# A transformer-like layer with gathered experts: the slots at which TensorE's pieces, the copies of its results and the choices are issued

## What is computed

```python
proj = rmsnorm(x, g_mix) @ w_in            # q | k | v | g (retention) | B | C | h (convolution)
o, ret_new = retention(ret_state, q, k, v) # chunked, with decay
c = gb * short_conv(gc * hc)
x = x + concat([rms_scale(o) * silu(g), c]) @ w_out
# peer: 8 heads; per token and head, 16 of 16,384 experts
q = rmsnorm(x, g_ffn) @ wq
s1, s2 = q[first half] @ keys1.T, q[second half] @ keys2.T
v1, i1 = top_k(s1, 16); v2, i2 = top_k(s2, 16)
top_s, sel = top_k(v1[:, None] + v2[None, :], 16); gate = softmax(top_s)
y = x + sum(gate * gelu(x . u[eidx]) * v[eidx])
y = rmsnorm(y, g_fin)
```

## Time and profile before

| what | value |
|---|---|
| median of 3 runs | 3299.9 us (3294.3 to 3301.84) |
| the profiled execution's own time | 3302.18 us, of which span 3300.4 us |
| first dot product, last dot product | 208.5 us, 3283.1 us |
| PE, DVE, ACT, POOL busy | 73%, 65%, 49%, 36% of the span |
| mean granted TensorE clock | 0.813 |
| moved by DMA | 1223.47 MB, mean 371 GB/s |

### The profile page before, as it was taken

One profiled execution on the slowest core, in us unless ns is written; L12 is line 12 of the kernel. 1 busy time (PEld: TensorE's weight loads), 2 busy tenths in 40 slices (PEclk: granted clock), 3 DMA queues, 4 the chain that ended last, 5 costly groups with the idle time before them and its releaser, 6 DMA issues.

```text
span 3300.4 us, 36101 instructions
## 1 busy us (share of the span) xinstructions
PE 2423.8 (73%) x12644; PEld 1993.6 (60%) x12644; DVE 2141.7 (65%) x6141; ACT 1607.1 (49%) x2626; POOL 1176.6 (36%) x1060
## 2 busy tenths in 40 slices
PE   8867787787776777787776887777766766667766
PEld 7656666656665666666665666655555655555555
DVE  1368875557888644556888744555788888555554
ACT  1135544455455544455455544456455455564455
POOL 0022333344443443334444333234443443444332
PEclk9978888797878888787878999888877777666666
DMA  6269998899999999899999999899999999999997
GB/s 238 79 255 358 375 374 328 310 403 402 415 387 416 383 420 394 317 388 401 418 395 414 369 421 408 320 340 373 419 403 374 366 384 367 412 417 421 421 421 320
DMA packets 183318, 1223.47 MB, mean 371 GB/s; under 512 B 21088, under 2 KB 26400, under 8 KB 43616
## 3 DMA queue, kind: packets, MB, share of 16 engines
q0 software_dynamic: 152064, 1107.36, 83.4%
q1 hardware_dynamic: 31072, 113.80, 9.1%
HBM read 1216.23 MB, written 4.86 MB: 370 GB/s over the span
## 4 chain that ended last, share of the span: by engine, by line
PE 39%; DVE 24%; DMA 18%; ACT 15%; issue 4%; POOL 0%; SPq 0%; DVEq 0%; ACTq 0%; POOLq 0%
DMA ring<-in_uv,idx 17%; PE expert_sum L813 14%; DVE ring L1094 10%; ACT ring L610 8%; PE mm L760 7%; PE mm L669 5%; PE mm L675 5%; PE x_ps L729 3%; DVE pairs_left L977 1%; ACT L621 1%; ACT dots L621 1%; DVE top_i L986 1%; DVE top_i L976 1%; PE tp L770 1%; DVE top_v L984 1%
## 5 line engine op out<-in xcount | busy, mean ns | idle before, releaser
L813 PE MATMUL expert_sum<-ident_sb,ring 128*128 128x128 f32 x8448 | 1486.3, 337 | 827.4 <-ACT ring L610 814.7
L474 POOL DMA_INDIRECT ring<-in_uv,idx x1056 | 1176.4, 1114 | 2094.6 <-PE expert_sum L813 1831.5
L813 PEld LDWEIGHTS expert_sum<-ident_sb,ring 128*128 128x128 f32 x8448 | 1235.1, 175 | 1086.2 <-ACT ring L610 1033.9
L1094 DVE CUSTOM_DVE_ANT_0 ring<-ring,xn 128x1024 f32<-128x1024 f32 x1056 | 1288.4, 1220 | 462.9 <-DMA ring<-in_uv,idx 454.5
L610 ACT ACTIVATE ring<-ring,weights 128x1024 f32<-128x1024 f32 x1056 | 1197.5, 1135 | 0.0
L621 ACT ACTIVATE dots<-dots 128x1 f32<-128x1 f32 x1056 | 211.5, 200 | 1065.2 <-DVE dots L1094 1061.9
L1076 DVE TENSOR_TENSOR weights<-dots,gate 128x1 f32<-128x1 f32 x1056 | 166.0, 157 | 166.5 <-ACT dots L621 166.2
L669 PE MATMUL mm<-stream,xn_in 128*128 128x256 f32 (+1 forms) x1024 | 255.6, 407 | 6.2 <-DVE xn_in L848 6.2
L760 PE MATMUL mm<-turn,stream 128*128 128x256 f32 (+1 forms) x1024 | 256.7, 407 | 0.7 <-ACT turn L554 0.7
L669 PEld LDWEIGHTS mm<-stream,xn_in 128*128 128x128 f32 (+1 forms) x1024 | 198.0, 199 | 47.8 <-DVE xn_in L848 6.6
L760 PEld LDWEIGHTS mm<-turn,stream 128*128 128x128 f32 x1024 | 204.8, 205 | 36.4 <-ACT turn L554 1.1
(11 more groups left out here) (158 smaller groups left out, 1541.7 us busy)
## 6 DMA issues: line engine op xcount, KB each, us to landing
stream<-in_w_ret SPq DMA_DIRECT2D x32, 1024.0 KB
stream<-in_wq SPq DMA_DIRECT2D x32, 1024.0 KB
stream<-in_w_conv SPq DMA_DIRECT2D x24, 1024.0 KB
ring<-in_uv,idx POOLq DMA_INDIRECT x1056
w_out_sb<-in_w_out SPq DMA_DIRECT2D x1, 4096.0 KB, 16.1
x<-in_x SPq DMA_DIRECT2D x8, 512.0 KB
out_y<-xn SPq DMA_DIRECT2D x8, 512.0 KB
xn_in<-in_xT SPq DMA_DIRECT2D x24, 128.0 KB
```

The costliest lines, as they stand in the source:

```text
L474: pool.indirect_dma_start(ring[:, g % RING, :], None, uv, bass.IndirectOffsetOnAxis(ap=rows, axis=0)).then_inc(landed[g % RING], 16)
L813: ins = pe.matmul(expert_sum[:, c * P:(c + 1) * P], ring[:, g % RING, D + c * P:D + (c + 1) * P], ident_sb[:, :], is_transpose=True, start ...
L1094: dve.tensor_tensor_reduce(u, u, xn[:, t % 3, :], 1.0, 0.0, ALU.mult, ALU.add, dots[:, g % RING:g % RING + 1]).then_inc(dotted, 1)
```

## The change

Only slot numbers change, with the order in which choices are made. The sums, sizes and buffers stay, except that the scores of SAMPLE get a place of their own in `qkvg`.

- A projection piece is issued over three slots (matmuls 0 to 2, 3 to 5, 6 and 7), every 4 slots; a query piece two matmuls a slot, its second half 4 slots behind the first. The four parts of retention's last products go to four slots.
- ScalarE and VectorE take a result two slots behind the end of its piece (before: one slot behind its only slot).
- Mixing has 22 slots for a tile (before 18) and begins 24 slots behind the first convolution piece in groups 1 and 2, 4 in groups 0 and 3.
- Heads of group 3 come every 15 slots (before 21), and SAMPLE's choices all behind those of tiles 6 and 7.

```diff
-RET_AT, RET_EVERY = 20, 9
-CONV_AT, CONV_EVERY = 92, 3.5
-MIX_AT, MIX_EVERY = 94, 18
-OUT_AT, OUT_EVERY = 138, 12
+USE_AT, USE_EVERY = 24, 4
+MIX_EVERY = 22
+def conv_at(j):
+    return base_of(j) + USE_AT + USE_EVERY * RET_UNITS * len(GROUPS[j])
+def mix_at(t):
+    j = group_of(t)
+    return conv_at(j) + (24 if j in (1, 2) else 4) + MIX_EVERY * place(t)
+def out_at(t):
+    j = group_of(t)
+    return max(mix_at(t) + 22, conv_at(j) + USE_EVERY * CONV_UNITS + 2 + 10 * place(t))
+def turn_at(t):
+    j = group_of(t)
+    return out_at(ORDERS[j][-1]) + 12 + 3 * place(t)
 def head_at(j, h):
     if j == 0:
-        return 13 * h - 18
-    return turn_at(j, len(GROUPS[j])) + 2 + (15 if len(GROUPS[j]) == 2 else 21) * h
+        return 13 * h - 26
+    return turn_at(ORDERS[j][-1]) + 5 + 15 * h
 def choose_at(j, h, i):
-    return head_at(j, h) + 5 + 7 * i
+    if GROUPS[j][i] == SAMPLE:
+        return choose_at(j, PH - 1, i - 1) + 7 * (h + 1)
+    return head_at(j, h) + 13 + 7 * i
...
         # TensorE, projection(j)
         for k in range(KC):
+            yield slot + k // 3
             ins = pe.matmul(bank[:, 0:w], item[:, unit % 2, k, :], xnj[:, k, :],
...
         # TensorE, queries(j)
-                yield head_at(j, h) + s
+                yield head_at(j, h) + 4 * s
         for k in range(KC):
+            yield head_at(j, h) + 4 * s + k // 2
             ins = pe.matmul(query_bank(j, s), weight[:, s, k, :], xnT_of_group(j)[:, k, :],
...
-                yield choose_at(j, h, i) - 2
+                yield head_at(j, h) + 10 + 7 * i if t < SAMPLE else head_at(j, h) + 13
...
         # ScalarE, projection(j); VectorE, conv(j) likewise
-                    yield slot + 1
+                    yield slot + 4
...
         # ScalarE, queries(j)
-                    yield head_at(j, h) + 2
+                    yield head_at(j, h) + 9
...
         # VectorE, choices(j)
-                for h in range(PH):
-                    for i, t in enumerate(GROUPS[j]):
+                pairs_of_tiles = [(h, i) for h in range(PH) for i in range(2)]
+                if SAMPLE in GROUPS[j]:
+                    pairs_of_tiles += [(h, 2) for h in range(PH)]
+                for h, i in pairs_of_tiles:
```

More of the change, by code:

```diff
@@ L100, in uses_of @@
         for i, t in enumerate(GROUPS[j]):
-            out.append(("ret", u, t, base_of(j) + RET_AT + RET_EVERY * u + RET_EVERY * i // len(GROUPS[j])))
+            out.append(("ret", u, t, base_of(j) + USE_AT + USE_EVERY * (u * len(GROUPS[j]) + i)))
     for v in range(CONV_UNITS):
-        out.append(("ChB"[v % 3], v, None, base_of(j) + CONV_AT + int(CONV_EVERY * v)))
+        out.append(("ChB"[v % 3], v, None, conv_at(j) + USE_EVERY * v))
     return out
@@ L152, in batches_of @@
         return [(0, 1), (2, 3), (4, 5), (6, 7)]
+    if t == SAMPLE:
+        return [(0, 7)]
     return [(0, 3), (4, 7)]
-GATES = sorted((j, last, i, first) for j in range(4) for i, t in enumerate(GROUPS[j]) for first, last in batches_of(t))
+GATES = sorted(((j, last, i, first) for j in range(4) for i, t in enumerate(GROUPS[j]) for first, last in batches_of(t)),
+               key=lambda b: pick(*b[:3]))
 def gates_ready(t, h):
@@ L261, in xn_of, with scores_of @@
             return xn[:, t % 3, :] if t < SAMPLE else xn_in[:, D:2 * D]
+        def scores_of(t, h):
+            if t < SAMPLE:
+                return scores[:, :, :]
+            return qkvg[:, 0, h * 2 * NK:(h + 1) * 2 * NK].rearrange("p (s k) -> p s k", s=2)
         def state_of(t):
@@ L440, in store_states @@
                 j = len(GROUPS) - 1
-                yield base_of(j) + OUT_AT
+                yield out_at(SAMPLE)
                 sp.wait_ge(tails_ready, 2 * CH)
@@ L518, in retention @@
                 n, r, j = rows_of(t), RANK[t], group_of(t)
-                at = base_of(j) + MIX_AT + MIX_EVERY * place(t)
+                at = mix_at(t)
                 yield at
@@ L540, in out @@
                 n, r, j = rows_of(t), RANK[t], group_of(t)
-                at = base_of(j) + OUT_AT + OUT_EVERY * place(t)
-                yield at + 9
+                at = out_at(t)
+                yield at + 10
                 act.wait_ge(x1_ready, r + 1)
@@ L731, in out @@
                 ins.then_inc(wout_done, 1)
-                yield turn_at(j, place(t))
+                yield turn_at(t)
                 pe.wait_ge(xn_ready, r + 1)
@@ L996, in choices @@
                                 dve.wait_ge(keyed_copied, c + 1)
-                            best16(tv[:, s, :], ti[:, s, :], scores[0:n, s, :], left[0:n, s * NK:(s + 1) * NK],
-                                   c + 1 if s else None)
+                            best16(tv[:, s, :], ti[:, s, :], scores_of(t, h)[0:n, s, :], left[0:n, s * NK:(s + 1) * NK],
+                                   pick(j, h, i) + 1 if s and t < SAMPLE else None)
                         yield at + 2
```

102 lines of the change are left out of this document (53 added, 49 removed).

## The result

The changed kernel takes 3121.45 us (median of four runs, 3118.02 to 3123.0) against 3300.87 us: ratio 0.9458, interval 0.9442 to 0.9474. The profiled execution has a span of 3121.2 us and a granted clock of 0.839 (before 0.813).

What follows compares the result with a forecast made beforehand. The prediction took gathers and weight loads (DMA) as the bound, with engine waits for pieces as excess. Gains 73 + 21 - 5 + 31 + 3 = 123 us from 3302 gave 3179, stated as 3178; range 3130 to 3265.

Steps and rivals of the forecast that it cites:

- The bound, and the rule to read a stage by: All slot stages: gathers at 2.52 us a slot plus 2.5 us per 1 MB of weights; time above is excess.
- Term 1: Mixing stages: waits for pieces mostly go, 3.0 us a slot; 73 us gained after 3 us back in each group.
- term 4: Choices: late query copies give 16 us in groups 1 and 2, group 3 gains 18, SAMPLE costs 3; together 31.
- the time ahead of slot 0: Before the first slot, more piece work ahead of TensorE's wait for `gated`: gain 3 us, bounds 0 and 6.
- Terms 2 and 3: First stage gains 21 us from spaced, spread pieces; weights loaded late, mostly in group 1, cost 5 us over all groups.
- the landing: Late weights: a load lands in 8 us against two slots, about 6 us, so each TensorE wait is 2 us.
- Ring buffers cover half: Late weights: ring buffers hide half of TensorE's waits for loads, leaving a cost of 5 us.
- the stage from 1857.6 us: Prepared stage to 2036.9 us, 64 slots and about 7 items: 179 us by the sum, took 179.3.
- The bank whose slack is gone: Rival: pieces behind slot 0 wait for the previous piece's copy, making the kernel slower, for example 3333 us; chance 0.06.
- The clock: Rival: thin parts lower TensorE's clock, making the kernel slower; at 0.55 it takes 3485 us; chance 0.04.
- Gain mostly spent again: Rival: late loads cost 84 us, or choices and mixing improve little; 3225 to 3293 us, centre 3255; chance 0.24.

Runs made afterwards that it cites:

- e7: Changed kernel with retention's steps back at their old slots (18 slots a tile, results taken one slot behind): 3118.6 us, ratio 0.9446.
- e14: e8 with retention's steps also put back (18 slots a tile, results taken one slot behind): 3242.9 us, ratio 0.9825.
- e8: e3 with mixing in groups 1 and 2 brought back to begin 4 slots behind the first convolution piece: 3221.6 us, ratio 0.9753.
- e3: Changed kernel with projection and query pieces whole again and their copies one slot behind, new table kept: 3203.3 us, ratio 0.9696.
- e10: Kernel before with late copies alone: projection copies three slots behind (before one), queries issued three slots sooner; spacing, mixing, whole pieces kept: 3159.9 us, ratio 0.9576.
- e1: Changed kernel with each projection and query piece and retention's last products whole in their first slot, copies left late: 3109.3 us, ratio 0.9410.
- e5: Changed kernel with group 1's units of retention projection nine slots apart (before eight), its convolution eight slots later: 3104.9 us, ratio 0.9403.
- e13: e1 with group 1's units of retention projection nine slots apart and its convolution eight slots later: 3103.8 us, ratio 0.9402.
- e4: Kernel before with only heads of group 3 every 15 slots (before 21) and SAMPLE's choices behind all others: 3278.8 us, ratio 0.9925.

## Why the prediction was right and wrong

**The bound, and the rule to read a stage by.** Right. Gathers and weights at 2.5 us a megabyte gave 136 us for a mixing stage; it took 139.2 and 139.7, at 419 GB/s. The excesses named were where the gain came from.

**Term 1, the mixing stages: the step that failed, in size and in its reason.** The time fell 9 us below the range, and no other term missed by as much. The prediction said "I don't give the stage the whole 35", took 3.0 us a slot, and gave back 3 us a group for mixing and `out` that end later. Measured are 2.90 us a slot, and in groups 1 and 2 no giving back but 4 to 5 us more behind the stage. In group 3 the 48 slots of 608 to 655 gained 44.3 us, but the 48 behind gave back 13.4, not 3, since the convolution had moved there; the term had priced the old stage as if it stayed in place. 101 us against 73 is half of the miss of 56; of the rest, term 4 has 10, what was not priced 12, and the time ahead of slot 0 5. The reason for holding back was retention's chain, which e7 shows to cost nothing once copies are late (with early copies its steps were worth 6 us, e14 against e8). And the wider spacing, the thin parts and "every copy and every h and B step falls two slots behind the end" were taken together as what makes the gain; e3 keeps it in groups 1 and 2 with neither thin parts nor late copies, e10 reaches it with late copies alone. In group 3, where three tiles share the stage and mixing lies over the convolution, the copies are what counts: 586.4 us in e3, 548.4 in e1.

**Terms 2 and 3.** The net, 18 against 17, is right by two errors, and so by luck. e1 has the ret and convolution pieces in the same slots and nearly no late weights (4.2 us of waits): 285.9 us. So the rest of the change is worth 31.6 us in this stage, not 21, and it is the late copies: alone they take 31.5 (e10), the table without them 1 (e3). Late weights cost 11 to 15 us over slots 0 to 175 (e1, e5 and e13 against the kernel after), not 4. The mis-sized part is the landing: 8 us were supposed, hence waits of 2 us; TensorE waited 28.1 us in six, up to 6.8 each, with two slots of lead (about 6 us). In the trace of e5, which has these landings, 1 MB takes 9.3 us from issue to landing for `in_w_ret` and 11.6 for `in_wq` and `in_w_conv` (medians over the span). "Ring buffers cover half" was not far off: from the kernel after to e1 24 us of waits go and 11 us of time, to e5 18 and 13. In groups 2 and 3 there was one such wait each, as foreseen, of 5.4 and 6.7 us; what they cost no run shows.

**Term 4.** 41 us against 31. In groups 1 and 2 it is 11 for 16, in group 3 29.5 for 15. The order of choices, to which I gave no share apart from the head spacing, is one of two changes that each take most of this excess. That SAMPLE's choices beside pure gathers would cost 3 us is about what shows: slots 848 to 911 took 164.6 us, before 162.2, and 159.6 in e4, where these choices end some 40 slots sooner.

**Not priced.** Slots 256 to 351 and 512 to 607 gained 11 us, nearly all in the latter, where three ret pieces stood in nine slots. With early copies slots 512 to 607 keep 275 and 276 us (e3, e14), with late copies in the old table 279 (e10); 276 before, 267 in the kernel after and 268 in e1. Here, then, neither cure does it alone; it takes both. I had read the stage from 1857.6 us, which lies within it and shows no excess, and passed over the 52.6 us of slots 528 to 543 just ahead. Ahead of slot 0 it was 8 us for 3, outside the bounds of 0 to 6: TensorE waited 1.76 and 0.98 us for `gated` instead of 3.92 and 3.75; e3 has 210.0 there and e1 198.5, so here too the copies count.

**Rivals.** The bank whose slack is gone cost next to nothing: 2.8 us of TensorE's waits for a copy ahead of a convolution piece in the whole span, in two waits. The clock: with the pieces in thin parts it was granted at 0.834 (e5), whole at 0.822 (e13), with equal times. The Trainium skill's advice in "TensorE: Matmul & The Clock Gate", "HAM oscillation — how this bites in real kernels", to keep the K-tiles of a piece together ahead of a wait, is not borne out where a slot's sum stands in each gap: the spread pieces have the higher clock. "Gain mostly spent again" named the loads rightly and put their price at 84 us, more than five times what it was.

## What to carry over

Where engines in fixed order share a fast inner loop, put each hand-over several rounds behind its producer, and look at that before breaking the producer's work into parts: here late copies alone made 141 of 179 us, and with copies four slots behind spreading added nothing (with copies one slot behind the end it was worth 58 us). Every slot by which a buffer is released later is taken from the lead of the load behind it: count the rounds from release to next use, since here two rounds (6 us) were too few and three nearly enough. Parts of a change that cure the same stall don't add up (late copies alone 141 us, the table and order without them 98 in e3, both together 192 in e1); price a stage by its distance from its bound, not by the waits removed one by one.

## What the runs showed that was not expected

- Four slots instead of 3.5 between pieces of 3.62 us took 15 us out of 48 slots (171.3 to 156.0, with the small shifts named at e14), although ten convolution pieces lie in these slots either way and the hand-overs stay one slot behind. No run shows why the half slot is worth so much.
- Waits of ScalarE and VectorE for pieces of 524 us in all (e3: 192.8, 77.4, 77.4, 77.1 and smaller), where e1 has 49, stand beside a time only 94 us longer. A sum of waits is no price.
